# A float32 decoder trunk on one core: output and down projections with the activations stationary and the residual kept by token

## The reference

```python
for i in range(DEPTH):                       # 2
    h = _rmsnorm(x, attn_norm_g[i])
    mix = _stick_breaking_attention(...) if i == 0 else _dsa_attention(...)   # both end in out @ w_o
    x = x + mix
    h = _rmsnorm(x, ffn_norm_g[i])
    x = x + _conv_ffn(h, ...)                # (silu(gate) * val) @ w_down, D_FF = 5632
```

## Time and profile before

| | us |
|---|---|
| median of 3 runs (2289.51 to 2294.32) | 2292.55 |
| span of the profiled execution, first to last instruction | 2287.3 |
| TensorE busy in it | 2261.3 (99%) |
| VectorE / ScalarE busy | 1514.6 (66%) / 1169.8 (51%) |
| DMA | 412 MB, mean 180 GB/s |

### The profile page before, as it was taken

One profiled execution on the slowest core, in us unless ns is written; L12 is line 12 of the kernel. 1 busy time (PEld: TensorE's weight loads), 2 busy tenths in 40 slices (PEclk: granted clock), 3 DMA queues, 4 the chain that ended last, 5 costly groups with the idle time before them and its releaser, 6 DMA issues.

```text
span 2287.3 us, 36356 instructions
## 1 busy us (share of the span) xinstructions
PE 2261.3 (99%) x13240; PEld 1991.1 (87%) x13240; DVE 1514.6 (66%) x1767; ACT 1169.8 (51%) x1401; POOL 2.6 (0%) x9
## 2 busy tenths in 40 slices
PE   7999999999999999999999999999999999999998
PEld 6999998888888888888888888888888888888887
DVE  6655656677777777555567888666777777774443
ACT  6555554555555555444454455555555555554332
POOL 0000000000000000000000000000000000000000
PEclk9999999999999999999999999999999999999999
DMA  6444545555556555555555544455556565555563
GB/s 224 157 166 158 167 160 182 176 188 190 188 180 201 182 194 190 187 192 185 190 189 165 172 154 139 135 194 173 190 181 201 178 198 190 186 191 197 201 194 120
DMA packets 113106, 411.99 MB, mean 180 GB/s; under 512 B 12688, under 2 KB 12816, under 8 KB 113040
## 3 DMA queue, kind: packets, MB, share of 16 engines
q1 hardware_dynamic: 111168, 404.80, 53.7%
q10 hardware_dynamic: 1296, 4.13, 0.5%
q0 software_dynamic: 576, 2.10, 0.3%
HBM read 408.88 MB, written 2.10 MB: 180 GB/s over the span
## 4 chain that ended last, share of the span: by engine, by line
PE 96%; DVE 3%; ACT 0%; issue 0%; ACTq 0%; POOL 0%; DVEq 0%
PE psum L944 96%; DVE w_lo L557 1%; DVE gates L569 0%; ACT w_hi L244 0%; DVE xg L565 0%; DVE rb L728 0%; PE psum L1141 0%; DVE tu L717 0%; DVE ra L733 0%; DVE tu L714 0%; DVE ra L726 0%; ACTq L291 0%; ACT pr L456 0%; DVE k_all L742 0%; DVE qr L742 0%
## 5 line engine op out<-in xcount | busy, mean ns | idle before, releaser
L557 DVE TENSOR_TENSOR w_lo<-raw,w_hi 128x1024 fp32r<-128x1024 f32 x772 | 937.9, 1223 | 709.6 <-ACT w_hi L244 703.3
L944 PE MATMUL psum<-xg,w_hi 128*128 128x512 f32 x3936 | 1379.5, 394 | 11.0 <-DVE xg L565 11.0
L244 ACT CAST w_hi<-raw 128x1024 fp32r<-128x1024 f32 x772 | 804.6, 1049 | 831.8 <-PE psum L944 831.2
L944 PE MATMUL psum<-xg,w_lo 128*128 128x256 f32 x3936 | 1103.3, 280 | 0.0
L944 PEld LDWEIGHTS psum<-xg,w_hi 128*128 128x128 f32 x3936 | 737.9, 187 | 176.4 <-DVE xg L565 11.3
L944 PEld LDWEIGHTS psum<-xg,w_lo 128*128 128x128 f32 x3936 | 745.1, 189 | 2.4 <-issue 2.2
L944 PE MATMUL psum<-hid,w_hi 128*128 128x512 f32 x1408 | 493.0, 393 | 0.0
L944 PE MATMUL psum<-hid,w_lo 128*128 128x256 f32 x1408 | 392.9, 279 | 0.0
L944 PEld LDWEIGHTS psum<-hid,w_hi 128*128 128x128 f32 x1408 | 263.8, 187 | 62.7
L944 PEld LDWEIGHTS psum<-hid,w_lo 128*128 128x128 f32 x1408 | 263.8, 187 | 0.0
L944 PE MATMUL psum<-att,w_hi 128*128 128x512 f32 x512 | 180.2, 394 | 0.0
(11 more groups left out here) (132 smaller groups left out, 961.5 us busy)
## 6 DMA issues: line engine op xcount, KB each, us to landing
raw<-w_all SPq DMA_DIRECT2D x772, 512.0 KB, 3.3
xres<-x_in ACTq DMA_DIRECT2D x4, 512.0 KB, 9.2
out_t<-xres POOLq DMA_DIRECT2D x4, 512.0 KB, 3.6
cst<-consts_in ACTq DMA_DIRECT2D x2, 768.0 KB, 9.3
vecs<-vecs_in ACTq DMA_DIRECT2D x1, 354.0 KB, 12.0
avg_d<-consts_in ACTq DMA_DIRECT2D x1, 64.0 KB, 11.7
vecs<-vecs_in ACTq DMA_DIRECT2D x1, 32.0 KB, 4.0
```

The lines of the kernel that those rows point to most:

```text
L244: act.copy(w_hi[:, c % RING, :], raw[:, c % RING, :]).then_inc(hi_ready, 1)
L557: dve.tensor_tensor(w_lo[:, c % RING, :], raw[:, c % RING, :], f32(w_hi[:, c % RING, :]), ALU.subtract).then_inc(lo_ready, 1)
L944: return pe.matmul(o, lhsT, rhs, start=start, stop=True, skip_group_check=True)
```

## The change

Seven edits go together.

1. In `out_groups` TensorE uses `proj_out` in place of `proj`: the activations (`att`, `hid`) are stationary and 512 columns of weights stream, three matmuls for each of 2 halves of the tokens and 2 tiles of features, 12 a piece. The result lies by token, 512 features in each of two banks.
2. The residual is `xtok` (128 tokens, 2, 2048 features). `add_group` is one addition of 128x1024 from PSUM into `xtok`; `copy_b` and the first addition are gone.
3. The next stage still needs x by feature: `turn` does 8 transposes of 128x128 float32 on TensorE into banks 4 and 5 for each group (m = 1, 2, 3), and `norm_hi` and `norm_lo` read PSUM. The turns of g = 0 to 2 stand behind piece 1 of the next group, that of g = 3 behind piece 0 of the next stage; ScalarE's and VectorE's parts moved to later pieces.
4. Squares are summed on ScalarE along a token's features (`accum_out`), two Squares of 512 columns a group.
5. The root and reciprocal work on 128x2. One plain float32 matmul of 256 columns of a matrix of ones with a diagonal of the reciprocals brings them into `rs` (`stat`), which VectorE copies (`spread`).
6. At the head x is loaded twice, by feature (`x_feat`, for the first norm) and by token (four more loads of 512 KB ahead of the constants on ScalarE's queue). The squares come after the wait for `cst`, behind the first and second split of `l0_pair`, and `stat(0)` stands behind piece 3.
7. The last piece's first half of tokens is signalled on its own, and the last quarter is added and stored in two halves.

```diff
+            def proj_out(c, b, src, k0_, first, split_end):
+                pe.wait_ge(lo_ready, c + 1)
+                s = c % RING
+                for th in range(2):
+                    for kk in range(2):
+                        w = slice(kk * 512, (kk + 1) * 512)
+                        x_hi = src[:, k0_ + kk, th * P:(th + 1) * P]
+                        x_lo = src[:, k0_ + kk, T + th * P:T + (th + 1) * P]
+                        mm(psum[:, b + th, :], x_hi, w_hi[:, s, w], first and kk == 0)
+                        mm(psum[:, b + th, :], x_hi, w_lo[:, s, w])
+                        last = mm(psum[:, b + th, :], x_lo, w_hi[:, s, w])
+                    if split_end and th == 0:
+                        last.then_inc(half_done, 1)
+                last.then_inc(piece_used, 1)
...
             def stat(m, bank):
-                pe.wait_ge(sqsum_ready, 4 * (m + 1))
...
+                pe.wait_ge(diag_ready, m + 1)
+                mm(psum[:, bank, 0:T], one, diag, True).then_inc(stat_ready, 1)
+            def turn(m, g):
+                pe.wait_ge(x_ready, 4 * (m - 1) + g + 1)
+                pe.wait_ge(xg_ready, 4 * m + g)
+                for kk in range(4):
+                    for th in range(2):
+                        k = 4 * g + kk
+                        last = pe.transpose(turned(kk)[:, th * P:(th + 1) * P], xtok[:, th, k * P:(k + 1) * P], eye)
+                last.then_inc(x_turned, 1)
...
                     for e in range(per):
                         if g == 0:
                             ready(e)
-                        proj(base + g * per + e, None, 0, 4 * (g % 2), src, 2, 2 * e, 512, e == 0)
+                        proj_out(base + g * per + e, OUT_BANK[g], src, 2 * e, e == 0, o == 15 and e == per - 1)
                         if tail and g == 0:
                             tail(e)
+                        if g and e == 1 and m < 4:
+                            turn(m, g - 1)
...
+                    if m is not None and e == 0:
+                        turn(m, 3)
                     if m is not None and e == 4:
-                        pe.wait_ge(acc_free, GROUPS * layer + 4)
-                        stat(m, 4)
+                        pe.wait_ge(xg_ready, 4 * m + 4)
+                        stat(m, TURN_BANK)
...
+            def squares(m, g):
...
+                for th in range(2):
+                    src = xtok[:, th, 512 * g:512 * (g + 1)].rearrange("p (a b) -> p a b", a=2)
+                    last = act.activation(conv[:, 2 * th:2 * th + 2, :], src, ACT.Square, accum_out=ss[:, th, g:g + 1])
+                last.then_inc(sq_ready, 1)
...
+            def recip(m):
                 dve.wait_ge(root_ready, m + 1)
+                dve.reciprocal(rs_tok[:, :], ssum[:, :]).then_inc(rt_ready, 1)
...
+                for th in range(2):
+                    last = dve.tensor_scalar(diag[:, th * P:(th + 1) * P], eye, rs_tok[:, th:th + 1], None, ALU.mult)
+                last.then_inc(diag_ready, 1)
+            def spread(m, bank):
+                dve.wait_ge(stat_ready, m + 1)
+                dve.tensor_copy(rs[:, :], psum[:, bank, 0:T]).then_inc(rs_ready, 1)
...
-                dve.tensor_tensor(part[:, :, :], psum[:, bank0:bank0 + 4, 0:T], part[:, :, :], ALU.add).then_inc(acc_free, 1)
...
-                dve.tensor_tensor(xres[:, 4 * g:4 * g + 4, :], xres[:, 4 * g:4 * g + 4, :], part[:, :, :], ALU.add).then_inc(x_ready, 1)
+                dve.tensor_tensor(xtok[:, :, c], psum[:, b:b + 2, :], xtok[:, :, c], ALU.add).then_inc(x_ready, 1)
```

More of the change, by code:

```diff
@@ L98, in build @@
             hid = sb("hid", [P, FT, 2 * T], F32R, mlp)
+        with ExitStack() as head:
+            x_feat = sb("x_feat", [P, KT, T], F32, head)
         att_ctx = ctx.enter_context(ExitStack())
@@ L322, in l0_pair @@
                         l0_ab(j - 1)
+                    if e < 2 and first:
+                        squares(0, 2 * e)
+                        squares(0, 2 * e + 1)
                     if e == 2 and first:
-                        root(0, 7)
+                        root(0)
                         act.preload_act_table_set("natural_log_exp_and_others")
@@ L413, in mlp_layer @@
                     if e == 0:
-                        norm(m, 3)
-                    if e == 4:
-                        root(m, 4)
+                        squares(m, 3)
+                    if e == 1:
+                        norm_hi(m, 3)
+                    if e == 2:
+                        root(m)
                         act.preload_act_table_set("silu_and_others")
@@ L474, in _ @@
                 if e == 0:
-                    norm(2, 3)
+                    squares(2, 3)
+                if e == 1:
+                    norm_hi(2, 3)
+                if e == 2:
                     act.wait_ge(cst_in, 32)
                     act.copy(idr[:, :], ident).then_inc(id_ready, 1)
+                    root(2)
+                    act.preload_act_table_set("natural_log_exp_and_others")
             evac(0, 0, 2, L1_QI0 + 3, None)
@@ L563, in norm @@
                 for k in range(4):
[L564 to L565 removed]
+                    dve.wait_ge(xhi_ready, 4 * n + (2 * (k // 2) + 2 if m else k + 1))
+                    src = turned(k) if m else x_feat[:, 4 * g + k, :]
+                    last = dve.scalar_tensor_tensor(out=xg[:, 4 * g + k, T:2 * T], in0=src, scalar=gain(m, 4 * g + k),
@@ L986, in out_groups @@
-            def out_groups(base, layer, per, src, n0, ready, tail=None):
-                for g in range(4):
-                    n = GROUPS * layer + n0 + g
-                    if g >= 2 or n0:
-                        pe.wait_ge(acc_free, n - 1)
+            def proj_out(c, b, src, k0_, first, split_end):
[12 more added lines that the diff above has]
+                last.then_inc(piece_used, 1)
@@ L992, in out_groups @@
+            def out_groups(base, m, per, src, ready, tail=None):
+                for g in range(4):
+                    o = 4 * (m - 1) + g
+                    if m % 2 == 0 and g < 2:
+                        pe.wait_ge(acc_free, UPG * m - 1 + g)
+                    if g == 2:
+                        pe.wait_ge(x_ready, o - 1)
                     for e in range(per):
@@ L1050, in l0_pair @@
                         l0_tri(j - 1)
-                    if e == 2 and first:
+                    if e == 3 and first:
                         stat(0, 7)
```

196 lines of the change are left out of this document (112 added, 84 removed).

## The result

The changed kernel takes **2308.83 us** (median of 4, 2308.06 to 2309.36). The kernel before, on the same chip, took 2291.05 (4 runs, 2289.51 to 2294.32). The ratio is **1.0074** (95% interval 1.0062 to 1.0086): slower by 0.74%, where 2284 was forecast. The profiled executions agree: the span is 2306.6 us, against 2287.3, so 19.3 us more, where -8.5 was the sum.

The account below looks back on a forecast made before the run. TensorE, busy 99% of the span, was taken as the bound. Terms -16.8 - 9.1 + 10.6 + 5.5 + 4.7 - 3.4 = -8.5 took the median 2292.55 to 2284 us, range 2276.5 to 2291.5.

Parts of the forecast that it names:

- The form of a piece: Output stages: 12 matmuls replace 16 for the same 6144 columns, saving 0.07 on each of 240 pieces, -16.8 us.
- I take 2.73, near the row of the same form: Output stages: new period per piece, 2.73 us, taken near the 2.72 of layer 1's value stage; before, 2.80.
- Rival (c): Output stages: columns alone set the period, which stays 2.80; slower, total 2301 us; chance 0.06.
- The statistics: `stat` for m = 1, 2, 3: from 3.51 us to 0.48, together -9.1 us.
- the turns: TensorE's 96 transposes over 3 norms and 4 groups, 0.11 us each, hidden by nothing: +10.6 us.
- Rival (d): The transposes in the norms drop TensorE's clock, making the kernel slower; chance 0.03.
- The waits: Changes of stage: 0.7 three times before g = 3's transposes, `stat` 1.0 twice, `xg` 1.1; together +5.5 us (2 to 8).
- The head: Start of kernel: `stat(0)` waits for squares held up by late constants (25.5), so piece 4 starts later: +4.7 us.
- four more issues of 0.47: Start of kernel, ScalarE's queue: added loads delay the first table load from 4.93 to 6.8, the first split to 8.1.
- The 1.7 us in 38.6: Start of kernel: last addend in piece 4's start, 36.4+0.5+1.7 = 38.6 us, compared with 34.0 before.
- The end: After the last piece: half an addition and a store of half the size, -3.4 us (-4.7 to -2.9).
- the 5.2 us from span to median: Whole kernel: median 5.2 us above the span of 2287.3, taken as untouched by the change and kept in the forecast.

Follow-up runs that it names:

- experiment 4: Changed kernel with 96 unused bytes ahead of `hid` and `att`, so both start at a multiple of 128: 2282.95 us, ratio 0.9977.
- experiment 6: Changed kernel, `xg` 32 past and `hid` at a multiple of 128: 2277.85 us; kernel before, `xg` 32 past: 2291.73 us, clusters 2287 to 2288, 2291 to 2293.

## Why the prediction was wrong

- **The form of a piece: wrong, and it is most of the miss.** Step: "I take 2.73, near the row of the same form". The count of matmuls was right, and so was the row, 2.72/12 = 0.227 us a matmul, but it had `xg`, at a multiple of 128, as its stationary operand. The place of the stationary operand sets the figure: 0.2267 us (0 past a multiple of 128), 0.2289 (64 past) and 0.2333 (32 past), that is 2.72, 2.75 and 2.80 a piece. Measured: 0 in place of -16.8. Rival (c) named the right outcome, 2.80 kept, for the wrong reason: columns alone do not set the period, as 2.72 shows in the same stage (experiment 4). It got 0.06, and its price, 2301, was 8 us short.
- **Layer 1's up loop: not in the sum at all.** The step that failed is the silent one, that an untouched loop keeps its pace: measured +9.0 in place of 0. The projections that stream `xg` have two paces, 2.77 and 2.83 a piece. In the profiled executions an up loop takes its pace by the turn and `stat` at its start and keeps it to its end. The kernel before had the slower one in parts of its layer stages (its stationary-`xg` stage aside), the changed kernel in layer 1's up loop.
- **The statistics, the turns: right.** `stat` is two records and costs 0.32 us and 0.19 more for the slow matmul behind it, where 0.48 was taken; a turn is 0.88 us, twelve of them. Rival (d) did not come about: the granted clock is 1.00 through the turns.
- **The waits: right in place, too small.** Before a turn of g = 3: 0.8 three times (0.7 forecast). `stat` in the MLPs: 1.46 where 1.0 was forecast, and `xg` in layer 1 1.2 where it was 1.1. Each of the three changes of stage cost 1.1 to 1.2 us more than the sum has for it; the longer waits are 0.2 to 0.6 of that, and the rest was not traced. All that is neither form nor up loop comes to 19.3 - 9.0 = +10.3, against 8.3 in the sum, 2 us over: 3.4 at the changes of stage and 0.65 in layer 0's first stage, less 1.65 in layer 1's attention and 0.35 in the head.
- **The head: right size, wrong path.** +4.35 against +4.7. The first split was put at 8.1 and came at 13.19, since the issue of the tenth load of the queue, of `idn`, took 4.39 us where its neighbours take 0.5 to 0.7. TensorE therefore began later and idled 4.9 us, not 10. The copy out of `cst` began at 24.83 (25.5 forecast), the root at 35.20 (about 35). The step "four more issues of 0.47" failed and was made up for by slack. That +4.35 is so near +4.7 is luck: a later start and a shorter idle stretch offset each other. The 1.7 us in 38.6 is a difference in the trace of the kernel before: its `stat(0)` took 5.22 us, at a granted clock of 0.50 in it, and the same `stat` 3.51 in the steady state. In the changed kernel the granted clock was 0.50 from 33.5 to 40.3 us, with TensorE at work from 36.34 on: 4.0 us at half the clock, an estimated 2.0 lost. That the first piece is slow by a low clock is not shown: its eight pairs took 5.29 us (17.21 to 22.50) at a granted clock of 1.00, and 5.28 before (10.24 to 15.52), also at 1.00.
- **The end: right**, -3.4.

With the two misses put right the sum would give 2284 + 16.8 + 9.0 = 2309.8, and 2308.83 was measured; two small errors nearly cancel in it. One is the 2 us above. The other is the 5.2 us from span to median, which the prediction took for what lies around the span. In every run whose span is on record the two are only 1.7 to 1.9 us apart, so the profiled execution took about 2289.1 us. It was one of the faster of the two groups of experiment 6, and the median, 2292.55, lies in the slower: that is the other 3.4 us, and they belong to the kernel before alone. The changed kernel has 2308.83 - 2306.6 = 2.2. More telling is experiment 4, the change with its operand in the place that the forecast took for granted: its span is 7.2 us below that of the kernel before, where -8.5 was the sum. That its median, 2282.95, lies so near 2284 is partly luck: the forecast holds the 3.4 us that should not be there, and five of the twelve runs lie at 2291 to 2292.

## What to carry to other kernels

A duration read off another stage carries that stage's operands with it: before a matmul's pace is moved to a new place, compare where the stationary operand starts in SBUF, and put the operands of the large products at multiples of 128 bytes if the runs of that kernel show what these do. Any change of small buffers moves all that is allocated behind them (here `hid` and `att` from 135904 to 136480), so a change that seems to cost in stages that it doesn't touch should be run with padding before it is judged. Moving a load earlier or onto another queue in a full stretch of transfers may only choose which buffer is late: here it gave 1.5 and 1.65 us where 4 and more were hoped for.

## What the runs showed of the hardware

- **The stationary operand's start.** Same instructions, float32r, 128x128 stationary and 512 columns moving, granted clock 1.00: 226.7, 228.9 and 233.3 ns a matmul (a piece of twelve at 2.72, 2.75 and 2.80 us) at 0, 64 and 32 bytes past a multiple of 128. 0 and 32 were seen with `xg` and with `hid` and `att`, in the value, output and down projections; 64 with `hid` and `att` alone. 96 past was not tried for a stationary operand.
- **The fixed part of a matmul.** At its best a matmul of 512 columns takes 226.7 ns, at a granted clock of 1.00. In the changed kernel's head, at 0.50, a pair of 512 and 256 columns takes 640 ns (three pairs from 38.00 to 39.92 us), with 0.43 us to the start behind the one of 512 and 0.21 behind the one of 256: by columns that is 427 for 512, and half of it, for twice the clock, is 213.3. So about 13 of the 226.7 ns don't go with the columns. That is an estimate from these two paces; no run separates it.
- **Two paces of one loop.** Pairs of 512 and 256 columns take 2.77 or 2.83 us for eight, with nothing else different that I found in the traces. With `xg` 32 bytes past a multiple of 128, no profiled execution of the new form (five kernels) had the slower one, and the runs of each agree within 2 us (one kernel ran once); at a multiple of 128 all five were slower in layer 0's first stage, by 1.8 to 3.6 us against those five, three of them had the slower pace in layer 1's up loop and one in layer 0's. What makes the pace switch at an interruption was not found.
- **A slow issue.** The tenth load issued by ScalarE took 4.39 us to issue, and 4.4 to 4.8 in the other kernels that left the order as it was; with four loads fewer ahead of it 0.47. Whether the number of loads or their bytes in flight sets this was not separated.
- **The clock comes back late at times.** After the same 3.4 us of idling of TensorE the granted clock was at 0.50 for 3.4 us in one execution and for 10.2 in another, with TensorE at work in both.
